# First feed-forward pair as a plain product on the unnormed residual; v of 16 tokens on four column groups

## The reference

```python
def _rmsnorm(x, gain):
    y = xf * lax.rsqrt(jnp.mean(xf * xf, axis=-1, keepdims=True) + RMS_EPS)
    return (y * gain.astype(F32_2)).astype(x.dtype)

def _swiglu(h, w_gu, w_down):                       # D_FF = 2816
    gate, up = jnp.split(h @ w_gu, 2, axis=-1)
    return (jax.nn.silu(gate) * up) @ w_down

h = h + _mixer_rglru_swa(_rmsnorm(h, ...), ...)     # layer 0
h = h + _swiglu(_rmsnorm(h, ffn_norm[0]), ...)
h = h + _mixer_retention(_rmsnorm(h, ...), ...)     # layer 1: 4 heads, v of 512 columns each
h = h + _swiglu(_rmsnorm(h, ffn_norm[1]), ...)
return h[:, N_META:]
```

## Time and profile before

| | us |
|---|---|
| three runs | 2664.03, 2663.0, 2669.01 (median 2664.03) |
| the profiled execution, its own time | 2664.31 |
| its span, first to last instruction | 2662.5 |
| TensorE busy in it | 2521.5 (95%), 11552 passes |
| VectorE, ScalarE, GpSimd busy | 944.9, 543.0, 149.8 |
| mean granted TensorE clock | 0.963 |
| products of the seven-product kind and other users of L1375, share of the chain | 38% |
| DMA | 307.12 MB, mean 115 GB/s |

### The profile page before, as it was taken

The page is one execution under the profiler, slowest core; times in us unless marked ns, Lnnn a source line. Parts: engine busy times, 40 slices in busy tenths (PEclk is TensorE's granted clock), DMA queues, the critical chain, the costliest instruction groups (busy, mean ns, idle before and its releaser), DMA issues.

```text
span 2662.5 us, 31031 instructions
## 1 busy us (share of the span) xinstructions
PE 2521.5 (95%) x11552; PEld 1905.3 (72%) x11552; DVE 944.9 (35%) x1671; ACT 543.0 (20%) x1121; POOL 149.8 (6%) x193
## 2 busy tenths in 40 slices
PE   7999999978999996989899999899999988999999
PEld 3564456567888875867788888665756777888888
DVE  7231266550000003363434542432342343435431
ACT  2300045421111113252211100112212111111100
POOL 1000054201111110000000000000000000000000
PEclk9999999878999998988999999899999999999999
DMA  9301121208989965201223222321220312222321
GB/s 332 103 15 56 38 97 72 80 34 324 330 329 328 332 238 193 62 26 48 64 79 94 81 64 95 111 72 44 75 69 26 95 40 95 80 88 85 89 87 46
DMA packets 83345, 307.12 MB, mean 115 GB/s; under 512 B 9264, under 2 KB 9264, under 8 KB 82624
## 3 DMA queue, kind: packets, MB, share of 16 engines
q1 hardware_dynamic: 75888, 274.24, 30.4%
q0 software_dynamic: 7376, 31.77, 3.0%
HBM read 292.86 MB, written 13.11 MB: 115 GB/s over the span
## 4 chain that ended last, share of the span: by engine, by line
PE 90%; DVE 4%; ACT 3%; issue 2%; DMA 1%; SPq 0%; DVEq 0%; POOL 0%; ACTq 0%; POOLq 0%
PE products L1375 38%; PE products L1222 9%; PE products L867 7%; PE products L1021 7%; PE products L1234 5%; PE products L1280 2%; PE products L1501 2%; PE products L1072 2%; PE products L1445 1%; PE products L931 1%; PE products L1330 1%; PE products L1150 1%; PE products L1040 1%; PE products L975 1%; PE products L882 1%
## 5 line engine op out<-in xcount | busy, mean ns | idle before, releaser
L1375 PE MATMUL products<-normed,ring 128*128 128x264 f32 (+1 forms) x1312 | 303.9, 388 | 11.3 <-DVE normed L2570 11.3
L1375 PEld LDWEIGHTS products<-normed,ring 128*128 128x128 f32 x1312 | 252.1, 193 | 56.1 <-issue 16.0
L1222 PEld LDWEIGHTS products<-arena,ring 128*128 128x128 f32 x2176 | 247.4, 193 | 8.8 <-issue 8.8
L1222 PE MATMUL products<-arena,ring 128*128 128x128 f32 x2176 | 247.7, 276 | 0.8 <-ACT arena L1744 0.8
L1597 ACT ACTIVATE arena<-products 128x512 f32<-128x512 f32 (+4 forms) x253 | 114.3, 471 | 621.7 <-PE products L1021 166.7
L1021 PE MATMUL products<-ring,normed 128*128 128x512 f32 (+1 forms) x416 | 182.5, 599 | 8.4 <-DVE normed L1954 8.4
L1375 PE MATMUL products<-arena,mixed 128*128 128x256 f32 (+1 forms) x832 | 189.4, 382 | 0.0
L1375 PEld LDWEIGHTS products<-arena,mixed 128*128 128x128 f32 x832 | 158.1, 190 | 23.8
L1375 PE MATMUL products<-normed,mixed 128*128 128x264 f32 (+1 forms) x704 | 161.5, 383 | 0.0
L1021 PEld LDWEIGHTS products<-ring,normed 128*128 128x128 f32 (+1 forms) x416 | 73.7, 178 | 115.8 <-issue 115.8
L1375 PE MATMUL products<-arena,normed 128*128 128x264 f32 (+1 forms) x704 | 155.6, 382 | 0.0
(11 more groups left out here) (443 smaller groups left out, 3166.5 us busy)
## 6 DMA issues: line engine op xcount, KB each, us to landing
ring<-in_weights SPq DMA_DIRECT2D x303, 512.0 KB, 4.3
ring<-in_experts SPq DMA_DIRECT2D x204, 512.0 KB, 5.1
arena<-results SPq DMA_DIRECT2D x8, 512.0 KB, 6.5
residual<-in_x POOLq DMA_DIRECT2D x1, 2048.0 KB, 15.8
arena<-in_dft_half POOLq DMA_DIRECT2D x1, 2048.0 KB, 8.4
token_rows<-arena SPq DMA_DIRECT2D x4, 512.0 KB, 2.8
out<-residual SPq DMA_DIRECT2D x8, 256.0 KB, 4.5
arena<-in_bias POOLq DMA_DIRECT2D x1, 1920.0 KB, 24.1
```

Of the source, the lines that this page charges most:

```text
L1222: m = pe.matmul(ps[:, side, m_ * P:(m_ + 1) * P], w[:, k, :], job_t[:, k, :], start=(k == 0), stop=(k == KT - 1))
L1375: m = pe.matmul(bank(p, n), left(k), right(k), start=(fresh and k == 0), stop=(k == kt - 1), skip_group_check=True)
```

## The change

- In both feed-forward layers the first of the 22 pairs is no longer a seven-product pair. TensorE computes it plainly, four products of eight feature tiles (gate and up, each for two token halves, banks 6, 3, 5, 4), on `raw_h`, x times gain without the root. ScalarE writes `raw_h` tile by tile beside the squares (`with_gain`). TensorE's program has the first of the four, then the product with ones (now in banks 7 and 2, or 7), then the other three.
- VectorE, after the norm and the four sums of halves, multiplies the two gate products by the root row, ScalarE takes their Silu, VectorE multiplies by the root row again and then by the up products, into `act_w[:, 0]`.
- 21 seven-product pairs follow: twelve in the loop, nine written out. Weight tile indices and semaphore counts shift by one pair. `settle` is replaced by a check that needs no waits.
- In retention, v of the last 16 tokens: feature tile k goes to column group k mod 4, that is to PSUM partitions 32 (k mod 4) on, so each group sums two tiles. VectorE copies the first group and adds the other three, in place of ScalarE's copy.

```diff
-FF_PAIRS, FF_LOOPED, FF_BODY = FFT, 12, 6
+FF_PAIRS, FF_LOOPED, FF_BODY = FFT - 1, 12, 6
...
-        r["ffn_ms", n] = b.many(halves)
-        r["before_ffn", n] = b.settle()
+        r["ffn_first", n] = [b.take(6)]
+        r["ffn_ms", n] = [b.take(x) for x in (7, 2)[0:halves]]
+        r["ffn_first", n] += [b.take(x) for x in (3, 5, 4)]
+        b.own_banks()
...
+        raw_h = [piece(arena, 11616, KT, T2), piece(arena, 14880, KT, S)]
...
-                w1 = k8(weights(name, 2 * i, it))
+                w1 = k8(weights(name, 2 * i + 2, it))
...
-                summed_square(sq_a if n == 0 else sq_b, r["ffn_ms", n], pieces, 2 if n == 0 else 4)
-                for b, v in r["before_ffn", n]:
-                    pe.wait_ge(bank_free[b], v)
+                raw = raw_h[n]
+                for i, p in enumerate(r["ffn_first", n]):
+                    if i % 2 == 0:
+                        w = k8(weights(name, i // 2))
+                    fill(p)
+                    for k in range(KT):
+                        if i == 0:
+                            pe.wait_ge(raw_ready, KT * n + k + 1)
+                        at = width * (i % 2)
+                        m = pe.matmul(bank(p, width), w[:, k], raw[:, k, at:at + width], start=(k == 0), stop=(k == KT - 1))
+                        if i % 2 == 0 and k == 0:
+                            begin(m)
+                    finish(p, m)
+                    if i == 0:
+                        summed_square(sq_a if n == 0 else sq_b, r["ffn_ms", n], pieces, 2 if n == 0 else 4)
...
-                    for t, p in enumerate(r["ret", "v"]):
-                        n = P if t < 4 else META
-                        token_major(p, lambda k, t=t, n=n: h2[:, k, t * P:t * P + n], w, n, t == 4, it)
+                    for t, p in enumerate(r["ret", "v"][0:4]):
+                        token_major(p, lambda k, t=t: h2[:, k, t * P:t * P + P], w, P, False, it)
+                    p = r["ret", "v"][4]
+                    fill(p, it)
+                    for k in range(KT):
+                        o = 32 * (k % 4)
+                        m = pe.matmul(ps[o:o + META, p.bank, :], h2[:, k, S:T2], w[k // 2][:, k % 2, :], start=(k < 4), stop=(k >= 4),
+                                      skip_group_check=True)
+                        if k % 2 == 0:
+                            begin(m)
+                    finish(p, m)
...
-                squares_of(x[:, :, t0:T2], sq_a if n == 0 else sq_b, T2 if n == 0 else S, whole)
+                raw, sq = raw_h[n], sq_a if n == 0 else sq_b
+                gain = par("norm_ffn")[:, 8 * n:8 * n + 8]
+                width = T2 if n == 0 else S
+                def square(k):
+                    act.activation(sq[:, k, 0:width], x[:, k, t0:T2], ACT.Square, scale=D ** -0.5).then_inc(squares, 1)
+                def with_gain(k):
+                    act.activation(raw[:, k], x[:, k, t0:T2], ACT.Copy, scale=gain[:, k:k + 1]).then_inc(raw_ready, 1)
+                if n == 0:
+                    for k in range(KT):
+                        whole(k)
+                        with_gain(k)
+                        square(k)
+                else:
+                    for k in range(4):
+                        whole(k)
+                        square(k)
+                    ready(act, r["ret_out"][2][P3])
+                    for k in range(4):
+                        with_gain(k)
+                    for k in range(4, KT):
+                        whole(k)
+                        with_gain(k)
+                        square(k)
                 root(r["ffn_ms", n], pieces, rstd)
                 w = HALF2 if n == 0 else S // 2
+                for i, p in enumerate(r["ffn_first", n][0:2]):
+                    read(act, p)
+                    act.activation(part_w[1][:, i, 0:w], part_w[1][:, i, 0:w], ACT.Silu).then_inc(wide_silu, 1)
...
-                    for t, p in enumerate(r["ret", "v"]):
-                        n = P if t < 4 else META
-                        copy(p, ret_v[0:n, t], ps[0:n, p.bank, :], it=it)
+                    for t, p in enumerate(r["ret", "v"][0:4]):
+                        copy(p, ret_v[:, t], bank(p), it=it)
...
+                g0, g1, u0, u1 = r["ffn_first", n]
+                gates = [part_w[1][:, j, 0:w] for j in range(2)]
+                rs = [rstd[:, 0:w], rstd[:, w:width]]
+                for j, p in enumerate((g0, g1)):
+                    ready(dve, p)
+                    tt_(gates[j], bank(p, w), rs[j], ALU.mult).then_inc(bank_free[p.bank], 1)
+                for j in range(2):
+                    dve.wait_ge(wide_silu, 2 * FFT * n + j + 1)
+                    link(tt_(gates[j], gates[j], rs[j], ALU.mult))
+                for j, p in enumerate((u0, u1)):
+                    ready(dve, p)
+                    tt_(act_w[:, 0, j * w:(j + 1) * w], bank(p, w), gates[j], ALU.mult).then_inc(bank_free[p.bank], 1)
                 with dve.Fori(0, FF_LOOPED // FF_BODY) as it:
                     for i in range(FF_BODY):
-                        gate_up(i, i, it * FF_BODY + i, r["ffn_loop", n][i], it)
+                        gate_up(i, i, it * FF_BODY + i + 1, r["ffn_loop", n][i], it)
                 for i in range(FF_LOOPED, FF_PAIRS):
                     seven = r["ffn_rest", n][i - FF_LOOPED]
-                    gate_up(i, i, i, seven)
-                    if i == FF_LOOPED:
-                        hidden_sums(0, seven)
-                    hidden_sums(i - FF_HALF, seven)
+                    gate_up(i, i, i + 1, seven)
+                    for k in range(0 if i == FF_LOOPED else i + 1 - FF_HALF, i + 2 - FF_HALF):
+                        hidden_sums(k, seven)
...
-                    me.loop(it, 17)
+                    me.loop(it, 20)
                     two_halves()
                     tile_sums_of(0, it)
                     tile_sums_of(1, it)
+                    p = r["ret", "v"][4]
+                    last = ret_v[0:META, 4]
+                    ready(dve, p, it)
+                    link(dve.tensor_copy(last, ps[0:META, p.bank, :]))
+                    for o in (32, 64):
+                        link(tt_(last, ps[o:o + META, p.bank, :], last, ALU.add))
+                    tt_(last, ps[96:96 + META, p.bank, :], last, ALU.add).then_inc(bank_free[p.bank], 1)
                     for j, name in enumerate(("q", "k", "g0", "g1")):
                         seven = r["ret", name]
                         p1, u2, p5 = (part_r[j % 2][:, i] for i in range(3))
```

More of the change, by code:

```diff
@@ L143, in settle, with own_banks @@
         return waits
+    def own_banks(self):
+        assert all(self.last[b] == (b, self.releases[b]) for b in range(8))
     def loop(self, n, turns, banks):
@@ L595, in two_blocks @@
         wide_silu = sem("wide_silu")
+        raw_ready = sem("x_with_gain_ready")
         tile_sums, half_sums, act_sums = sem("weight_tile_sums"), sem("token_half_sums"), sem("hidden_half_sums")
@@ L1402, in gate_up @@
                 product(seven[P3], 4, width, lambda k: s[:, 3, k], lambda k: h2[:, 4 + k, width:2 * width], it)
-                w2 = k8(weights(name, 2 * i + 1, it))
+                w2 = k8(weights(name, 2 * i + 3, it))
                 pe.wait_ge(half_sums, 4 * n + 4)
@@ L1428, in ffn @@
                         summed = 4 * (4 * n + j)
-                        w = [k8(weights(name, 44 + 6 * j + s, it)) for s in range(6)]
+                        w = [k8(weights(name, 2 * FFT + 6 * j + s, it)) for s in range(6)]
                         begin(product(seven[P1], H, width, rows_of(w[0], w[3], 0), lambda k: act_w[:, k, 0:width], it, fresh=True))
@@ L2496, in pair_sums @@
                 def pair_sums(i, pair, it=None):
-                    first = name + 2 * i
+                    first = name + 2 * i + 2
                     for t in (first, first + 1):
@@ L2513, in gate_up @@
                     p1, u2, p5 = (part_w[i % 2][:, j, 0:w] for j in range(3))
-                    silus = 2 * (FF_PAIRS * n + pair)
+                    silus = 2 * (FFT * n + pair + 1)
                     ready(dve, seven[P2], it)
@@ L2545, in row_sums @@
                 def row_sums(g):
-                    first = name + 2 * FF_PAIRS + 6 * g
+                    first = name + 2 * FFT + 6 * g
                     for t in range(first, first + 6):
```

## The result

| | us |
|---|---|
| kernel before, median of 4 | 2666.52 (2663.0 to 2669.57) |
| changed kernel, median of 4 | 2631.62 (2628.78 to 2632.59) |
| ratio | 0.9868, 95% interval 0.985 to 0.9885 |
| the profiled execution after, its own time; its span | 2630.67; 2628.8 |

The account below looks back on a forecast made before the run. TensorE was taken to bound the kernel, by its passes plus the places where it stands still. Gains of 8.0 + 8.6 + 20.0 = 36.6 us took 2664.0 to 2627.4, range 2623 to 2638.

Parts of the forecast that it names:

- Layer 0, forecast 8.0: First feed-forward layer's start: the plain first pair fills the gap behind the output product, gaining 8.0 us, bounds 5 to 8.6.
- Of it 2.3 is clock: First feed-forward layer: 2.3 of the 8.0 us is clock, as pair 0 took 14.8 us instead of 12.5.
- Layer 1, forecast 8.6: Second feed-forward layer's start: the same plain first pair gains 8.6 us with a stall of 1.0, bounds 5 to 9.6.
- The rest ... nothing: Remaining feed-forward pairs and output tail: three hidden sums instead of two, 1.7 us on an idle VectorE, cost nothing.
- v of 16 tokens, forecast 20.0: Retention: four column groups streaming at once cut the product from 7.1 to 2.1 us, 5.0 per head, 20.0 in four.
- the changes of mode: Retention, both sides of the narrow v product: switching between 128-wide and narrow passes costs about 0.4 us.
- Rival 1: Retention's v: groups stream only two at a time, or weight loads come into the open; 13.6 us saved, 2634; chance 0.19.
- rivals 2 and 4: Retention's v: groups run one after another, 2647.4, chance 0.08; or each group change empties the array, 2674, chance 0.03.
- The factor of 3.07: Retention's v: the skill's speedup for four row groups, by which passes take an estimated 2.2 us, not 1.72; sum 2 less.
- the longer runs hide the start: Retention's v: runs of four passes per group hide the start, so the skill's lower speedup was not used.
- Rival 3: Both feed-forward layers: table loads in the chain or VectorE falling behind give back 9 us, 2636; chance 0.06.
- The sum: Whole kernel: 8.0 + 8.6 + 20.0 = 36.6 us gained, from 2664.0 to 2627.4.

Follow-up runs that it names:

- e8: Kernel before with idle products of 128 columns ahead of and behind the ones product in each feed-forward layer, filling the gap; 2667.93 us, ratio 1.0.
- e5: Changed kernel with the two bank triples of the feed-forward pairs exchanged, so the down product's P1 finds its bank free; 2628.99 us, ratio 0.9866 to before.
- e1: Changed kernel with v of the last 16 tokens undone, on one group and copied by ScalarE as before; 2652.11 us, ratio 0.9939 to before.
- e2: Kernel before with only v of the last 16 tokens put on four column groups and added by VectorE; 2648.01 us, ratio 0.9913.
- e3: Changed kernel with v's eight contraction tiles on two column groups instead of four; 2635.61 us, ratio 0.9883 to before.
- e4: Changed kernel with the same four column groups, but both tiles of a group one after the other in program order; 2639.23 us, ratio 0.9896 to before.
- e6: As e5, with VectorE multiplying the plain pair's two gate products by the root before the last two sums of halves; 2628.91 us, ratio 0.9852 to before.
- e7: Changed kernel with the ones product behind the plain pair's second product instead of its first; 2639.93 us, ratio 0.9898 to before.

## Why the prediction was right, and where it was not

- **Layer 0, forecast 8.0.** From the free point of the stream to pair 1 less the stop: forecast 15.7 us (1302.7 - 1286.96), measured (P6's stream at 1307.97 less 3.56) 1304.41 - 1288.73 = 15.7. The way there was right too: norm start 7.1 us after the free point forecast and 7.2 measured, gate multiplication 17.6 and 17.6, stop 0.6 and 0.55. ScalarE's copy with gain takes 0.74 us, not 0.64, hidden as the square is.
- **Its split, "Of it 2.3 is clock", was wrong.** e8 shows 0.5, since the slow passes lay beside VectorE's norm and sums. The sum did not hang on it, since it went by absolute times, but a reader who had filled the gap for the clock's sake would have gained 0.5 us and not 2.3. What the plain pair does is to put 14 us of work that needs no norm beside the norm chain, of which the slow passes were a part.
- **Layer 1, forecast 8.6**: 2241.57 - 3.45 - 2222.66 = 15.5 us against the forecast 2264.0 - 2248.34 = 15.7.
- **"The rest ... nothing" failed.** With 21 seven-product pairs instead of 22 the last one is on banks 0 to 2, the same as the down product's P1, whose first pass must wait for VectorE's last multiplication. I had followed the banks of the plain pair and the added hidden sums, but not the parity at the loop's other end. It costs 0.8 us in each layer: from the ab output's free point to retention's ones product 425.3 (1712.26 - 1286.96) became 418.0 (1706.71 - 1288.73), 7.3 instead of 8.1, and in layer 1 8.0 instead of 8.8. e5 shows the cause. The hidden sums themselves cost nothing.
- **v of 16 tokens, forecast 20.0**: 5.13 us per head, 20.5 in four; e1 and e2 have 20.5. The term was 0.5 us too small: 1.84 us from the product's first pass to q's where I had 2.1, against 6.97 before (1863.38 - 1856.41) where I had 7.1. Twelve slots of 0.43 fewer would be 5.16 us and the period fell by 5.13, so the changes of mode cost hardly more than before; I had allowed 0.4 us for them. Rival 1 (two at a time, or loads in the open) and rivals 2 and 4 are out by e3 and e4: the eight pass slots of two groups, the four of four, and no visible load. The factor of 3.07 that the Trainium skill (TensorE: Matmul & The Clock Gate, "Measured speedup vs the span model") gives for four row groups did not bind for these four column groups: 16 passes in four rounds of 0.43 us are the full four. I had argued that the longer runs hide the start; the rounds do follow each other without a pause, but no run here has a single pass per group to compare. What that section's model says, that further tiles cost almost nothing beside the stream's length, is what these rows show, with four starts within 0.02 us.
- **Rival 3** (part of the gain given back at the chain's end) did not come: the chain holds no further table load than the one between Ln and Exp that was there before (Ln at 1292.94 follows its product as before, the Silu's load at 1295.93 lies beside the norm), and the stops have the size forecast (0.55 and 0.8 against 0.6 and 1.0).
- **The sum.** 8.1 + 8.8 - 1.6 + 20.5 = 35.8, the stretches say 35.5; forecast 36.6. The 0.3 us between them is clock: the first head, behind the gap before retention, gained 4.9 us and not 5.13, and retention's output product took 0.1 us longer. That the sum is within 1.1 us of the forecast is in part luck: the 1.6 us that I had missed is half made up by terms that were 0.1, 0.2 and 0.5 us too small.

## What to carry to other kernels

Where a norm's root is one factor per token, the first product behind it can run on the unnormed input and be scaled afterwards; here the work so freed (14.2 us), the ones product and pair 1's first two products (3.6 us) nearly covered the chain from the norm to the copy of P1, and stops of only 0.55 and 0.8 us were left. The reduction that starts the chain should not stand later than it must: one product later cost 10 us here. When the number of turns of a loop changes, look at what the last turn leaves behind (its banks), not only at what the first one meets. A product with few stationary columns can be spread over column groups by its contraction tiles: its time here was that of the fullest group's passes, for the price of a few additions on an engine that was idle.

## What the runs showed of the hardware that was not expected

- The order of the groups' passes in the program has no effect on how they overlap, over 16 passes (e4: 1.93 us with all four passes of a group adjacent, 1.91 interleaved).
- The same gap gives back the clock at different times. TensorE idles 8.36 to 8.39 us before retention in every kernel; behind it the first 64 v passes took 30.63 us in the changed kernel (clock 0.74 in 1720 to 1724), 29.33 in e5 and 29.12 in e6 (1.00 there), while e6's ones product ahead of the gap fell into the low clock and took 2.13 us for 1.16. The first 32 passes of retention's output product, behind a stop of 5.2 us, took 9.22 us in the changed kernel, 8.60 in e5 and 10.18 in e6. Nothing in the code differs there. Together these places make e5 1.9 us faster and e6 0.4 us slower than their code accounts for, so changes under some 2 us can't be read from one execution's span or stretch, and are better read from the part that they touch.
- A stop of 3.84 us (e7) was followed by a granted clock of 0.67, stops of 0.28 to 0.53 us by none below 1.00 (the windows from 1302 us of the changed kernel). The stop of 2.62 us before retention's ones product was followed by 1.00 in the changed kernel (1704 to 1708) and by 0.73 in e6 (the same window).
